# Moving expert rows through DRAM: whole 4 KB rows with 6 + 6 indirect DMAs in place of quarter rows with 24 + 24

## The reference

```
logits = h @ w_router                       # h: the 288 normed rows of 1024
top_val, top_idx = top_k(logits, 2)
gates = softmax(top_val)
y[t] = x[t] + sum over the 2 chosen e of  gates[t, e] * ((silu(h[t] @ Wg[e]) * (h[t] @ Wu[e])) @ Wd[e])
# Wg, Wu: 1024 x 3584, Wd: 3584 x 1024, 44 MB an expert, 352 MB in all
```

## Time and profile before

| | |
|---|---|
| median of the timed runs | 1475.06 us (1471.85 to 1477.02) |
| span of the profiled execution, which is the time shown for it | 1520.8 us |
| PE busy | 95% of the span |
| expert stage | 587 us to 1511.6 us |
| DMA | 470 MB, mean 309 GB/s; some 415 GB/s in experts 1 to 6 |
| POOL busy | 10%; 24 indirect DMAs from 590.6 us and 24 from 1395.3 us |

### The profile page before, as it was taken

The page is one execution under the profiler, slowest core; times in us unless marked ns, Lnnn a source line. Parts: engine busy times, 40 slices in busy tenths (PEclk is TensorE's granted clock), DMA queues, the critical chain, the costliest instruction groups (busy, mean ns, idle before and its releaser), DMA issues.

```text
span 1520.8 us, 35582 instructions
## 1 busy us (share of the span) xinstructions
PE 1451.5 (95%) x16137; PEld 1036.0 (68%) x16137; DVE 442.1 (29%) x927; ACT 305.0 (20%) x551; POOL 158.0 (10%) x201
## 2 busy tenths in 40 slices
PE   7998999999989888899999999999999999998798
PEld 6885899999978464367567566576576675674145
DVE  6765656655667543000010000000000000010031
ACT  5435544434444353000000000000000000000000
POOL 1322130000012243200000000000000000002300
PEclk9999999999999899899999999999999999999799
DMA  9638786535744256699999999999999999999493
GB/s 324 220 103 272 258 321 199 160 115 160 254 134 145 85 224 249 218 373 417 418 408 418 414 415 418 409 416 419 406 419 419 407 418 419 408 417 403 160 394 135
DMA packets 162522, 470.37 MB, mean 309 GB/s; under 512 B 10304, under 2 KB 102848, under 8 KB 133440
## 3 DMA queue, kind: packets, MB, share of 16 engines
q1 hardware_dynamic: 154016, 438.62, 74.8%
q0 software_dynamic: 8352, 29.43, 5.5%
HBM read 450.32 MB, written 17.69 MB: 308 GB/s over the span
## 4 chain that ended last, share of the span: by engine, by line
PE 87%; DVE 6%; issue 3%; DMA 1%; ACT 1%; SPq 0%; POOL 0%; DVEq 0%; ACTq 0%
PE psum L1094 40%; PE psum L1134 19%; PE psum L331 7%; PE psum L332 7%; PE psum L333 7%; DVE wlo L327 2%; PE psum L804 2%; PE psum L730 1%; PE psum L865 1%; ACT whi L323 1%; PE psum L739 1%; DVE hl L1481 1%; PE psum L789 0%; DVE hn L1477 0%; PE psum L844 0%
## 5 line engine op out<-in xcount | busy, mean ns | idle before, releaser
L1094 PE MATMUL psum<-wexp,xg 128*32 128x512 f32 (+1 forms) x6144 | 614.4, 544 | 24.8 <-issue 23.7
L1094 PEld LDWEIGHTS psum<-wexp,xg 128*32 128x32 f32 x6144 | 330.6, 110 | 296.5 <-issue 221.8
L1134 PE MATMUL psum<-wexp,act 128*32 128x256 f32 x5376 | 296.6, 379 | 0.0
L1134 PEld LDWEIGHTS psum<-wexp,act 128*32 128x32 f32 x5376 | 220.0, 110 | 74.2 <-issue 1.7
L1909 DVE TENSOR_TENSOR am<-sg,psum 128x512 f32<-128x512 f32 (+1 forms) x48 | 26.9, 617 | 817.5 <-PE psum L1094 817.5
L331 PE MATMUL psum<-hh,whi 128*128 128x288 f32 x696 | 212.0, 305 | 2.8 <-DVE wlo L327 2.8
L332 PE MATMUL psum<-hl,whi 128*128 128x288 f32 x696 | 206.2, 296 | 0.0
L333 PE MATMUL psum<-hh,wlo 128*128 128x288 f32 x696 | 205.9, 296 | 0.0
L327 DVE TENSOR_TENSOR wlo<-raw,whi 128x2048 fp32r<-128x2048 f32 (+1 forms) x66 | 140.3, 2127 | 69.9 <-ACT whi L323 69.9
L331 PEld LDWEIGHTS psum<-hh,whi 128*128 128x128 f32 x696 | 131.7, 189 | 9.2 <-issue 4.6
L332 PEld LDWEIGHTS psum<-hl,whi 128*128 128x128 f32 x696 | 131.7, 189 | 1.2
(11 more groups left out here) (307 smaller groups left out, 1061.1 us busy)
## 6 DMA issues: line engine op xcount, KB each, us to landing
wexp<-in_w_moe SPq DMA_DIRECT2D x224, 1024.0 KB, 10.9
wexp<-in_w_moe SPq DMA_DIRECT2D x128, 768.0 KB, 10.3
raw<-in_w_gu_dense SPq DMA_DIRECT2D x22, 1024.0 KB, 5.2
wexp<-in_w_moe SPq DMA_DIRECT2D x32, 512.0 KB, 10.8
raw<-in_w_qkv_a SPq DMA_DIRECT2D x12, 1024.0 KB, 12.3
raw<-in_w_down_dense SPq DMA_DIRECT2D x16, 704.0 KB, 4.7
raw<-in_w_q_b SPq DMA_DIRECT2D x6, 1024.0 KB, 5.2
keys_a<-in_cache_a_k SPq DMA_DIRECT2D x20, 256.0 KB, 3.2
```

The costliest lines, as they stand in the source:

```text
L1094: ins = nc.tensor.matmul(ps[NG * part + r][32 * j:32 * j + 32, 0:wd], xg[:, r, 32 * k:32 * k + 32], wexp[:, q % RING, wd * j:wd * j + wd], ...
L1134: ins = nc.tensor.matmul(ps[6 + r // 2][32 * j:32 * j + 32, 256 * (r % 2):256 * (r % 2) + 256], act[:, r, 32 * kk:32 * kk + 32], wexp[:, q ...
```

## The change

The DRAM tensors hold rows whole: `h_rows` is (13, 96, 1024) and not (13, 128, 3, 256). An indirect DMA moves 128 (or 32) rows of 4 KB. The index of a row is its slot alone, so the arithmetic for quarters goes from VectorE's route. In exchange the block of an expert, which must be cut into quarters for the 32-partition bands, is stored and loaded by four direct DMAs of 96 KB each (32 partitions, 3 pieces of 1 KB each) in place of one of 384 KB (128 partitions, 3 KB each). The clearing of the tensors with zeros keeps its 128 x 3 KB form. Semaphore counts follow.

```
-        h_rows = nc.dram_tensor("h_rows", (NBLK, P, NG, 256), F32, kind="Internal").ap()
+        h_rows = nc.dram_tensor("h_rows", (NBLK, CAP, D), F32, kind="Internal").ap()
...
+        def quarter(rows, n, j):
+            return rows[bass.ds(n, 1), :, 256 * j:256 * j + 256].rearrange("b (r s) d -> s (b r) d", r=NG)
...
                         eng.wait_ge(sem("out_copied"), 2 * n + 2)
-                        eng.dma_start(o_rows[bass.ds(n, 1)].rearrange("b p r d -> p (b r) d"), out_rows[:, :, :])\
-                            .then_inc(sem("last_stored" if last else "out_stored"), 16)
+                        for j in range(4):
+                            eng.dma_start(quarter(o_rows, n, j), out_rows[32 * j:32 * j + 32, :, :])\
+                                .then_inc(sem("last_stored" if last else "out_stored"), 16)
...
-                        eng.wait_ge(sem("rows_moved"), 384)
+                        eng.wait_ge(sem("rows_moved"), 96)
                         eng.wait_ge(sem("xg_ready"), n + 1)
-                        eng.dma_start(xgs[:, :, :], h_rows[bass.ds(h_next, 1)].rearrange("b p r d -> p (b r) d")).then_inc(sem("xg_loaded"), 16)
+                        for j in range(4):
+                            eng.dma_start(xgs[32 * j:32 * j + 32, :, :], quarter(h_rows, h_next, j)).then_inc(sem("xg_loaded"), 16)
...
                 for i in range(2):
-                    for j in range(4):
-                        nc.gpsimd.indirect_dma_start(h_parts, bass.IndirectOffsetOnAxis(ap=rowi[0:w, i, c, j:j + 1], axis=0),
-                                                     htok[0:w, c, 256 * j:256 * j + 256], None).then_inc(sem("rows_moved"), 16)
+                    nc.gpsimd.indirect_dma_start(h_flat, bass.IndirectOffsetOnAxis(ap=rowi[0:w, i, c:c + 1], axis=0),
+                                                 htok[0:w, c, :], None).then_inc(sem("rows_moved"), 16)
...
-            V.tensor_scalar(s3(7), pslot[:, :, :], 2 * CAP + 0.5, None, ALU.is_gt)
-            chain(V.scalar_tensor_tensor(out=s3(6), in0=s3(8), scalar=-float(CAP), in1=pslot[:, :, :], op0=ALU.mult, op1=ALU.add))
...
+            chain(V.tensor_scalar(rowf[:, 2:4, :], rowf[:, 0:2, :], float(CAP), None, ALU.add))
```

More of the change, by code:

```diff
@@ L275, in build_program, with whole @@
         tab = at("tab", 96192, [P, 16], I32)
-        h_rows = nc.dram_tensor("h_rows", (NBLK, P, NG, 256), F32, kind="Internal").ap()
-        o_rows = nc.dram_tensor("o_rows", (NBLK + 1, P, NG, 256), F32, kind="Internal").ap()
-        h_parts, o_parts = (x.rearrange("b p r d -> (b p r) d") for x in (h_rows, o_rows))
+        h_rows = nc.dram_tensor("h_rows", (NBLK, CAP, D), F32, kind="Internal").ap()
+        o_rows = nc.dram_tensor("o_rows", (NBLK + 1, CAP, D), F32, kind="Internal").ap()
+        h_flat, o_flat = (x.rearrange("b s d -> (b s) d") for x in (h_rows, o_rows))
+        def whole(rows, i):
+            return rows[i].rearrange("s d -> (s d)").rearrange("(p n) -> p n", p=P)
+        def quarter(rows, n, j):
+            return rows[bass.ds(n, 1), :, 256 * j:256 * j + 256].rearrange("b (r s) d -> s (b r) d", r=NG)
         T_E, T_H, T_N = 0, OVER + 1, 2 * OVER + 2
@@ L431, in _ @@
                     eng.wait_ge(sem("zeros_ready"), 1)
-                    eng.dma_start(o_rows[NBLK], zeros[:, :, :]).then_inc(sem("out_stored"), 16)
+                    eng.dma_start(whole(o_rows, NBLK), zeros[:, :, :].rearrange("p r d -> p (r d)")).then_inc(sem("out_stored"), 16)
             def expert_piece(e, q):
@@ L634, in _ @@
                 for i in range(2):
-                    for j in range(4):
-                        nc.gpsimd.indirect_dma_start(h_parts, bass.IndirectOffsetOnAxis(ap=rowi[0:w, i, c, j:j + 1], axis=0),
-                                                     htok[0:w, c, 256 * j:256 * j + 256], None).then_inc(sem("rows_moved"), 16)
-            eng.wait_ge(sem("rows_moved"), 384)
-            eng.wait_ge(sem("last_stored"), 16)
+                    nc.gpsimd.indirect_dma_start(h_flat, bass.IndirectOffsetOnAxis(ap=rowi[0:w, i, c:c + 1], axis=0),
+                                                 htok[0:w, c, :], None).then_inc(sem("rows_moved"), 16)
+            eng.wait_ge(sem("rows_moved"), 96)
+            eng.wait_ge(sem("last_stored"), 64)
             for i in range(2):
                 for c, (t0, w) in enumerate(TB):
-                    for j in range(4):
-                        nc.gpsimd.indirect_dma_start(mixed[i][0:w, c, 256 * j:256 * j + 256], None, o_parts,
-                                                     bass.IndirectOffsetOnAxis(ap=rowi[0:w, 2 + i, c, j:j + 1], axis=0)).then_inc(sem("rows_moved"), 16)
+                    nc.gpsimd.indirect_dma_start(mixed[i][0:w, c, :], None, o_flat,
+                                                 bass.IndirectOffsetOnAxis(ap=rowi[0:w, 2 + i, c:c + 1], axis=0)).then_inc(sem("rows_moved"), 16)
             for b in "ab":
@@ L1859, in _ @@
             V.tensor_tensor(s3(8), s3(4), s3(10), ALU.mult)
             chain(V.tensor_tensor(s3(9), s3(5), s3(10), ALU.mult))
[L1861 to L1867, removed]
@@ L1868, in _ @@
[L1868 to L1870 removed]
+            V.tensor_reduce(rowf[:, 0, :], s3(8), AXX, ALU.add)
+            chain(V.tensor_reduce(rowf[:, 1, :], s3(9), AXX, ALU.add))
+            chain(V.tensor_scalar(rowf[:, 2:4, :], rowf[:, 0:2, :], float(CAP), None, ALU.add))
@@ L1915, in expert @@
                     if half == 1 and last:
-                        eng.wait_ge(sem("rows_moved"), 768)
+                        eng.wait_ge(sem("rows_moved"), 192)
                         eng.wait_ge(sem("x_rows"), 6)
```

21 lines of the change are left out of this document (8 added, 13 removed).

## The result

The kernel got slower: 1484.91 us, the median of 8 runs (1478.6 to 1491.34), against 1475.12 for the kernel before beside it (8 runs, 1471.85 to 1481.75). The ratio is 1.0069 [1.0049, 1.0088]. The forecast was 1474 and no change; what came is rival C, and within a microsecond or two its 1486.

A forecast was written before the change was run, and what follows sets the result against it. PE was taken to bound the kernel, with the weight stream hardly having anything to spare. All terms were valued 0 in timed runs: 1475.06 + 0, about 1475, said as 1474 for small gains; range 1464 to 1486 (own range 1470 to 1480).

The forecast's parts named there:

- rival C: Late experts: split transfers cost over 0.7 us each, the weight stream becomes the bound, PE waits; 1486 us, chance 0.15.
- the price of the split loads: DMA engines, band loads and stores: +0.2 to +0.9 us a transfer, bounds -0.2 to +5.4; hidden, so valued 0.
- Cover: Down-stage weight loads: needed 23 us after issue, landing after 12.7 us in expert 6, so 10 us left to hide delays.
- The crawl: PE's slow matmuls in expert 0 and the last, while GpSimd issues: 48.5 us, taken as only in the profiled execution.
- Rival B: Expert 0 and the last: PE's 48.5 us of slow matmuls are in timed runs too and go; 1430 us, chance 0.18.
- It isn't missing instructions: PE's slow matmuls, expert 0: the instruction queue moved nothing in 596 to 624 us, so PE had its code.
- The profiled span, 1472: Whole profiled execution: 1520.8 less the 48.5 us of slow matmuls, so 1472 us.
- Indirect DMAs, 30 to 7.5 us of GpSimd: GpSimd, scatter and gather: 24 issues of 1.25 us become 6 at each place; valued 0 in timed runs.
- SP held by the scatter: SP, expert 0: weight loads held 12 us at `rows_moved`, not held after the change; covered by 12 pieces in hand, 0.
- rival D: The 12 us hold at `rows_moved` reaches PE or late experts, and the change returns 5 to 10 us; 1467, chance 0.10.
- Route, -1.8 us: VectorE: 9 fewer instructions of 0.18 to 0.22 us bring the scatter forward by 1.8 us; off the path, 0.
- Rival E: GpSimd: a whole-row indirect DMA takes four times as long to issue; time as forecast, chance counted within the forecast's 0.57.

The follow-up runs named there:

- before_groups: The kernel before, its one load of the next expert's rows cut into three DMAs of 1 KB rows over all 128 partitions: 1475.53 us, ratio 1.0008.
- before_stride: The kernel before, its load of the next expert's rows cut into four DMAs of 32 partitions, each taking every fourth partition: 1474.51 us, ratio 1.0005.
- after_again: The changed kernel run again unchanged: 1482.71 us against 1474.6 for the kernel before, ratio 1.0052.
- before_again: The kernel before run again unchanged, with a profile beside its timed runs: 1474.19 us.
- mixed_fourth: The kernel before with only the gather side changed (four band stores, 6 indirect DMAs): 1496.99 us against 1520.07, ratio 0.9847.
- bands_spread: The changed kernel, its four band loads ordered 0, 2, 1, 3, one behind each weight load of pieces 20 to 23: 1482.74 us against 1521.72, ratio 0.9754.
- load_again: The changed kernel, each expert's rows loaded by one DMA over 128 partitions (rows misplaced): 1475.0 us beside 1474.6 for the kernel before.
- loads_by_group: The changed kernel, each expert's rows loaded by three DMAs over 128 partitions instead of four bands: 1486.12 us against 1521.95, ratio 0.9775.
- both_by_group: The changed kernel, rows both loaded and stored by three DMAs over 128 partitions instead of four bands: 1510.53 us, ratio 0.9925.

## Why the prediction was wrong

**The step that failed** is the price of the split loads: "I take +0.2 to +0.9, nearer to the row with the stream". It was +2.8 us in the load of expert 2, and 1.4 to 3.6 in the seven, 20.9 us in all. The bounds of the text held it (-0.2 to +5.4), and so did the rule for what comes through: 7 x 2.8 - 10 = +10. The row it was taken from, 349 GB/s, is a load of 1 MB in pieces of 1 KB and no narrow one. It priced the DRAM side, which does cost next to nothing (before_groups, 1.0008). The sentence that a DMA of 32 partitions may load the SBUF side unevenly, and that no row shows one, named the right place and then gave it no weight. A term with no row of its own and a cover of only 0.7 us a transfer should have moved far more than 0.15 of the chance to rival C.

**The rule that was weighed and set aside.** The prediction read the rule of the Trainium skill (DMA: Bandwidth & Descriptors, section Rules for kernel authors) against two transfers to disjoint partition ranges as a fixed cost that overlaps, and so it does: four DMAs of spread partitions are free (before_stride). What cost time here is the place of the partitions, not the count of the DMAs.

**Rival C** came as written, in place and sign: late experts, landing times over 20 us, PE waiting for `wexp` from expert 4 on, 1486 us. That its number came so close is luck: +1.5 us for each of 14 transfers was an example and no measurement, and 14 x 1.5 = 21 us happens to be what 7 loads cost (20.9), with little for the stores.

**Cover.** "Issued when a slot comes free and needed 23 us later" was right: experts with landing times of up to 22.7 us show no wait, and in after_again, where the loads of expert 2 land after 23.8 us, the first wait comes in expert 3 already.

**The crawl, in timed runs 0.** The number was right for the chip of the comparison; the reason, "the crawl belongs to the profiled execution", was wrong. The run before_again has a profile without it beside timed runs of 1474, and on three other occasions the kernel before took 1520 to 1522 us in timed runs. As far as seven comparisons on six chips can say, it goes with the chip that a kernel meets: the one chip that was met twice, half an hour apart, had it both times. So the argument "where could a timed run save 45.7 us?" had an answer that the text didn't think of: in running elsewhere. Rival B is true on those chips (mixed_fourth gives back 23.1 us by half of the edit, bands_spread 39.0 by all of it less the bands) and false on the others. That the profile of before came from one of those chips is likely from its span, but nothing records it.

**"It isn't missing instructions"** is weaker than it was put. In 596 to 624 us the instruction queue moved nothing, but in before_again, in the same stretch and with the same DMAs, it moved this:

```profile
q8 instruction: 2, 0.03, 0.4%
```

So the instruction queue brought two packets beside a PE at full pace, and none beside a crawling one. Whether their lack starts the crawl or follows from it no run here tells.

**The profiled span, 1472:** the crawl went from the profile as said, but the span fell to 1489.7 and not to 1472. The expert stage went from 924.6 to 885.8 us, which is the crawl's 48 less the 9 that the bands cost, and expert 0 starts 7.6 us later (594.57 against 587.02), which is scatter between executions: in after_again it starts at 585.98.

**Indirect DMAs, 30 to 7.5 us of GpSimd:** right. The six scatters are issued from 596.59 to 603.83. **SP held by the scatter:** right and covered. before_again shows the hold, 10.6 us where 12 were forecast, and load_again, without it, lands its weights 3 us sooner (10.9 against 13.9) in the same time, which also refutes rival D:

```profile
SPq L476 <- DMA h_rows<-htok,rowi: 10.6, 1, 10.6
```

**Route, -1.8 us:** the first scatter comes 2.0 us behind expert 0's start in place of 3.6. **Rival E** is refuted by the 0.87 to 1.06 us of each whole-row DMA.

## What to carry to other kernels

When one transfer is cut into several, look at the SBUF partitions that each part writes before counting DMAs or bytes a row: beside a stream that fills the engines, parts of 32 or 64 neighbouring partitions took a quarter to a third of its rate for some 12 us (320 and at worst 266 GB/s of 415), and parts with every fourth partition took nothing. If a stream has only microseconds in hand, an operation that no row of the profile shows should carry a good part of the chance at its upper bound. When the profiled time and the timed runs differ by 3%, ask first whether they come from the same chip: profile and times agreed within 0.5% wherever one chip gave both.

## What the runs showed of the hardware

- The same 24 + 24 indirect DMAs of GpSimd stall PE's issue to one matmul in 0.7 us on some chips and not at all on others. Of the six chips that the experiments met two have it, one of them met twice: 1520 to 1522 us against 1473 to 1475 for the same kernel. Each side of 24 costs some 24 us there, and 6 cost 0 to 1.4 us (bands_spread, loads_by_group, both_by_group, mixed_fourth).
- A window can show the DMA engines fully busy at 266 GB/s. So the share alone doesn't tell the rate: 1.03 stands beside 266 GB/s in the changed kernel and beside 418 in before_stride.
- An indirect DMA of 4 KB rows is issued as fast as one of 1 KB rows (0.87 to 1.06 us for up to 128 rows).
- SP's issue of a 128 KB load took under 0.7 us with 128 outermost on the DRAM side and 3.5 us with 4 (1.99 us for three in before_groups, 10.46 in both_by_group). Three stores with 4 outermost took 2.91 us in expert 1 and 19.29 in expert 2, so more than the shape sets it.
